# mLSTM scan of a two-block mixer: gate rows loaded from memory, the minimum on ScalarE, the next step's mask first, numerators in two pairs of banks in turn

## The chip, the cores and the metric

The kernel is one program on one core of a Trainium2 chip. The metric is the time of the whole program on the device in microseconds, as the median of several executions. Its engines are TensorE (PE in the profile, with PEld for its weight loads), VectorE (DVE), ScalarE (ACT), GpSimd (POOL) and SyncE (SP, which here only issues transfers). Each has a program of its own and they meet by semaphores. Every matmul writes to PSUM, eight banks of 2 KB a partition, called `ps` here.

## The reference

Two transformer blocks over 512 latent and 256 context tokens, in fp32. The change lies in the first mixer of the second block, in its mLSTM half: four heads of 128, in chunks of 128 tokens, once forward and once backward, the two results added. With the gates' logarithms given, a step of one direction is:

```
bcum = jnp.cumsum(fc, axis=-1)
d_log = jnp.where(lower, bcum[..., :, None] - bcum[..., None, :] + ic[..., None, :], -jnp.inf)
inter_log = bcum + m[..., None]
m_t = jnp.maximum(inter_log, jnp.max(d_log, axis=-1))
inter_w = jnp.exp(inter_log - m_t)
s = jnp.einsum('bhtd,bhsd->bhts', qc, kc) * jnp.exp(d_log - m_t[..., None])
num = inter_w[..., None] * jnp.einsum('bhtd,bhde->bhte', qc, c_mat) + jnp.einsum('bhts,bhse->bhte', s, vc)
den = inter_w * jnp.einsum('bhtd,bhd->bht', qc, n_vec) + jnp.sum(s, axis=-1)
h = num / jnp.maximum(jnp.abs(den), jnp.exp(-m_t))[..., None]
...
c_new = carry_w[..., None, None] * c_mat + jnp.einsum('bhs,bhsd,bhse->bhde', w, kc, vc)
n_new = carry_w[..., None] * n_vec + jnp.einsum('bhs,bhsd->bhd', w, kc)
```

## The kernel before, in words

The program is a series of blocks. Inside a block the engines run side by side; between two blocks all of them wait for one another. The second block's first projection (L1292) makes queries, keys, values and gates, unit by unit. While it runs, `Gates` turns the 16 gate columns into rows of 4 heads by 2 directions by 768 tokens and computes on them the running sums and maxima: `row_i` (for each token what stands for `inter_log - m_t`), `row_m` and `row_b`. TensorE then transposes them back to columns, per chunk (L3612), and after that goes on with the projection. The columns are `rp` (for each key token what is added to a query's row), `em`, `i_cols` and `w_all`.

The scan is a block of its own (L3799 and on), in twelve steps. `order_m` names direction `d` and chunk `c` of each; the directions alternate. In steps 0, 1 and 4 to 7 the chunk is met for the first time (`seen[s]` is false), in 2, 3 and 8 to 11 the other direction has been there. A step s goes so:

- TensorE (`front`): `bc`, the row of `row_i` of each head broadcast to all 128 partitions by a matmul of a broadcast column with the identity (L3804), and `cols`, the scores of keys and queries (L3811), into banks 0 and 1 or 2 and 3 by the parity of s.
- ScalarE: `iw`, the exponential of the broadcast rows (L3921). GpSimd multiplies the queries by it (`qs`, L3943) and the keys by `w_all` (`kw`, L3946).
- VectorE (`seg`): minimum of row plus `rp` column and zero (L3854, one for each head); ScalarE: exponential in place (`p_exp`, L3923); VectorE (`masked`): times the triangular mask (L3862), times the scores (L3865), `m`.
- TensorE (`p`): numerators and denominators, from the masked scores with the values (L3830) and from `qs` with the state (L3831), always into banks 4 and 5; then products for the state (`masked`, L3841) into banks 6 and 7.
- VectorE: the denominators, two operations and a reciprocal (L3878 to L3881, signalled as `rd`). If the chunk is new, ScalarE copies the numerators out with the reciprocal as scale (`give`, L3913); if not, VectorE adds them to what is there (L3886) and ScalarE squares the sum (L3790). Then VectorE brings the state forward (`mem`, L3898).

Each engine's instructions run in the order in which they are written. VectorE's order in iteration s is: minimum of s+1, denominators of s, addition of s, mask of s+1, state of s. ScalarE's is: `iw` of s, `p_exp` of s, `give` of s-1. TensorE's is: `front` of s+1, numerators of s, state products of s. Behind the last step ScalarE applies a sigmoid to the output gate (L3932) and loads the table of the square root (L3933). The next block is the band attention.

## Time and profile before

| | |
|---|---|
| median of 3 runs | 2406.1 us (2403.95 to 2406.68) |
| profiled execution, its own time | 2406.52 us |
| its span in the trace | 2404.7 us |
| TensorE busy | 2295.4 us (95%) |
| VectorE busy | 1256.0 us (52%) |
| ScalarE busy | 802.0 us (33%) |
| GpSimd busy | 971.5 us (40%) |
| mean granted TensorE clock | 0.98 |

The span is that of the trace, and the execution's own time has the start and end around it. Busy times count an engine's instructions without its waits; the busy share says little of a block whose engines wait for each other, so the block of the scan is read by itself, in the timeline and in windows. In a timeline row the first number is the start, the second the time from the start of the group's first instruction to the end of its last, and the bracket holds the idle time before it and the instruction that ended it. TensorE's fp32 matmuls show as two records each.

### The profile page before, as it was taken

The numbers are of one execution on the slowest core, as the hardware profiler recorded it, in microseconds if no ns is written. First come the engines' busy times: TensorE is split into PE (matmuls) and PEld (weight loads), VectorE is DVE, ScalarE is ACT, GpSimd is POOL, SyncE is SP. The second block draws the span as 40 slices with busy tenths as digits, with TensorE's granted clock in tenths as the row PEclk, the third lists the DMA queues.
The fourth block names the chain that finished last, engine by engine and source line by source line (L and its number), as shares of the span: only waits on it lengthen the run. The fifth ranks groups of instructions, "written<-read, shape, count | busy, mean of one in ns | idle before, by whom it ended". The sixth has DMA issues, their size and how long they took to land. (4 is left out here: it accounts for less than half of the span.)

```text
span 2404.7 us, 34304 instructions
## 1 busy us (share of the span) xinstructions
PE 2295.4 (95%) x14079; PEld 1901.3 (79%) x14079; DVE 1256.0 (52%) x2102; ACT 802.0 (33%) x1406; POOL 971.5 (40%) x639
## 2 busy tenths in 40 slices
PE   6999889999998999978999999999999998999999
PEld 5877757788776789855888888888877787888887
DVE  3647468756646660579165695755239651411111
ACT  4444353333325312356231121211143462322222
POOL 1236325555552222326234352534422133645653
PEclk8999989999999999989999999999999999999999
DMA  8325235535543111100112334343212002323321
GB/s 272 107 93 189 88 106 179 170 119 162 171 145 116 36 53 53 37 1 8 47 53 66 127 106 140 106 139 105 71 45 70 19 3 69 104 89 105 103 77 47
DMA packets 227577, 228.31 MB, mean 95 GB/s; under 512 B 7439, under 2 KB 225507, under 8 KB 227427
## 3 DMA queue, kind: packets, MB, share of 16 engines
q1 hardware_dynamic: 227091, 226.09, 29.4%
q8 instruction: 109, 1.79, 0.3%
q14 instruction: 41, 0.34, 0.0%
q10 hardware_dynamic: 336, 0.11, 0.0%
HBM read 224.08 MB, written 2.10 MB: 94 GB/s over the span
## 5 line engine op out<-in xcount | busy, mean ns | idle before, releaser
L1661 POOL TENSOR_TENSOR w_lo<-ring,w_hi 128x1024 fp32r<-128x1024 f32 x124 | 303.8, 2453 | 353.7 <-ACT w_hi L1655 353.7
L2633 DVE SCALAR_TENSOR_TENSOR xT<-ps,mods,xT 128x512 f32<-128x512 f32 (+1 forms) x160 | 107.6, 682 | 460.7 <-PE ps L1738 411.2
L1655 ACT ACTIVATE w_hi<-ring 128x1024 fp32r<-128x1024 f32 x124 | 130.7, 1058 | 490.9 <-PE ps L1738 490.9
L1736 PE MATMUL ps<-hidden_hi,w_hi 128*128 128x512 f32 (+1 forms) x768 | 272.6, 355 | 0.6 <-POOL hidden_lo L3023 0.6
L1737 PE MATMUL ps<-hidden_lo,w_hi 128*128 128x512 f32 (+1 forms) x768 | 272.0, 354 | 0.0
L2926 DVE SCALAR_TENSOR_TENSOR ffn_sums<-ps,cols,ffn_sums 128x441 f32<-128x441 f32 (+2 forms) x352 | 215.0, 687 | 108.9 <-ACT ffn_sums L2845 108.9
L1738 PE MATMUL ps<-hidden_hi,w_lo 128*128 128x512 f32 (+1 forms) x768 | 271.7, 354 | 0.0
L1736 PE MATMUL ps<-h_hi,w_hi 128*128 128x512 f32 (+1 forms) x720 | 255.5, 355 | 0.0
L1737 PE MATMUL ps<-h_lo,w_hi 128*128 128x512 f32 (+1 forms) x720 | 255.0, 354 | 0.0
L1738 PE MATMUL ps<-h_hi,w_lo 128*128 128x512 f32 (+1 forms) x720 | 254.7, 354 | 0.0
L2868 POOL TENSOR_TENSOR ffn_w_lo<-ring,ffn_w_hi 128x1024 fp32r<-128x1024 f32 (+2 forms) x76 | 161.7, 2130 | 215.8 <-ACT ffn_w_hi L2818 215.8
L1292 PE MATMUL ps<-h_hi,w_halves 128*128 128x512 f32 (+1 forms) x560 | 203.6, 364 | 7.6 <-DVE ab_lo L676 2.9
L3013 DVE TENSOR_TENSOR squares<-squares 128x512 f32<-128x512 f32 (+1 forms) x72 | 87.8, 1219 | 162.0 <-ACT squares L2999 162.0
L1271 POOL TENSOR_TENSOR ring_low<-ring,w_halves 128x1024 fp32r<-128x1024 f32 x31 | 74.7, 2417 | 228.4 <-ACT w_halves L1265 228.4
L1736 PEld LDWEIGHTS ps<-hidden_hi,w_hi 128*128 128x128 f32 x768 | 145.2, 189 | 22.3 <-POOL hidden_lo L3023 1.1
L1738 PEld LDWEIGHTS ps<-hidden_hi,w_lo 128*128 128x128 f32 x768 | 145.2, 189 | 20.2
L1737 PEld LDWEIGHTS ps<-hidden_lo,w_hi 128*128 128x128 f32 x768 | 145.2, 189 | 20.0
L2818 ACT ACTIVATE ffn_w_hi<-ring 128x1024 fp32r<-128x1024 f32 (+2 forms) x76 | 71.9, 947 | 250.5 <-PE ps L2807 234.3
L1736 PEld LDWEIGHTS ps<-h_hi,w_hi 128*128 128x128 f32 x720 | 136.1, 189 | 20.7 <-issue 1.2
L1737 PEld LDWEIGHTS ps<-h_lo,w_hi 128*128 128x128 f32 x720 | 136.2, 189 | 18.8
L1738 PEld LDWEIGHTS ps<-h_hi,w_lo 128*128 128x128 f32 x720 | 136.1, 189 | 18.9
L1068 DVE SCALAR_TENSOR_TENSOR h<-ring,sil,h 128x256 f32<-128x256 f32 x196 | 131.6, 695 | 5.0
(489 smaller groups left out, 5194.7 us busy)
## 6 DMA issues: line engine op xcount, KB each, us to landing
ring<-in_mlp_w SPq DMA_DIRECT2D x64, 1024.0 KB, 5.4
ring<-in_ada_w SPq DMA_DIRECT2D x48, 1024.0 KB, 5.4
ring<-in_w_ada SPq DMA_DIRECT2D x24, 1024.0 KB, 5.4
ring<-in_ffn_w_up SPq DMA_DIRECT2D x22, 1024.0 KB, 5.3
ring<-in_ab_w_in SPq DMA_DIRECT2D x11, 1024.0 KB, 5.3
ring<-in_ffn_w_down SPq DMA_DIRECT2D x12, 768.0 KB, 4.8
ring<-in_w_in SPq DMA_DIRECT2D x8, 1024.0 KB, 8.6
ring<-in_c_w_in SPq DMA_DIRECT2D x6, 1024.0 KB, 5.0
```

The source lines that it names most:

```text
L1068: ins = dve.scalar_tensor_tensor(acc, slab, s, acc, ALU.mult, ALU.add)
L1271: pool.tensor_tensor(low_half(h), ring_half(h), w_halves[:, h % 3, :, :].bitcast(F32), ALU.subtract)\
L1292: ins = pe.matmul(o, stationary, moving, start=(k == 0 and i == 0), stop=(k == KT - 1 and i == 2))
L1655: act.activation(w_hi[m][:, 0:x["kt"], :], ring[:, x["n"] % NS, 0:x["kt"], m * P:(m + 1) * P], ACT.Copy).then_inc(SW["w_hi"].sem, 1)
L1661: pool.tensor_tensor(w_lo[m][:, 0:x["kt"], :], ring[:, x["n"] % NS, 0:x["kt"], m * P:(m + 1) * P], w_hi[m][:, 0:x["kt"], :].bitcast(F32), ...
L1736: pe.matmul(o, w_hi[m][:, k, :], h, start=(k == 0), stop=False)
L1737: pe.matmul(o, w_hi[m][:, k, :], l, start=False, stop=False)
L1738: ins = pe.matmul(o, w_lo[m][:, k, :], h, start=False, stop=(k == x["kt"] - 1))
L2633: return nc.vector.scalar_tensor_tensor(x, bank, column_of(gates, t * 2 + 2 * gate + r), x, ALU.mult, ALU.add)
L2868: pool.tensor_tensor(w_lo[i % NW][:, 0:kt, :], ring[:, n % NS, 0:kt, m * P:(m + 1) * P], w_hi[i % NW][:, 0:kt, :].bitcast(F32), ALU.subtract)\
L2926: ins = dve.scalar_tensor_tensor(o, on_grid(ps[:, (first + m) % 4, :])[:, y0 + dy:y1 + dy, x0 + dx:x1 + dx], cols[:, CW + tap * 2 * FT + t ...
L3013: dve.tensor_tensor(sq, sq, sq, ALU.mult).then_inc(v_order.sem, 1)
```

## The change

The rows no longer come from TensorE. ScalarE's queue stores `row_i` to memory once, when the rows are complete; SP loads for each step the four heads' rows of the step's chunk into all 128 partitions, 256 KB a step, into six buffers in turn (`row_in`): two steps ahead of the last slab of the projection's stage, four at the block's start, and the rest as buffers come free. `iw` reads that buffer. The transposes of `row_i` and the column `i_cols` go; `rp_neg`, the negative of `rp`, takes its place. The minimum is made on ScalarE as Relu of (-row - rp), and the exponential takes its negative. VectorE's order becomes: mask of s+1, denominators of s, addition of s, state of s. Numerators of even steps go to banks 4 and 5, those of odd steps to 0 and 2, which the broadcasts have left. The squares are written into the row buffer as scratch. VectorE waits for the store before it sets the ones column of the values, which share memory with `row_i`.

```diff
@@ Gates
+        row_in = [big[:, rows_at + b * 512:rows_at + (b + 1) * 512].rearrange("p (h n) -> p h n", h=4)
+                  for b in (NR - 2, NR - 1, *range(NR - 2))]
+        def load_rows(sp, s):
+            d, c, _ = order_m[s]
+            sp.dma_start(row_in[s % NR], gate_rows[:, d, c * CH:(c + 1) * CH].partition_broadcast(P))\
+              .then_inc(row_loaded[s // 2 % (NR // 2)].sem, 16)
...
-                            for i, row in enumerate((row_m, row_b, row_i)):
+                            for i, row in enumerate((row_m, row_b)):
                                 pe.transpose(ps[:, 4, i * N4 + o:i * N4 + o + 4], row[:, d, cut], ident[0:4, 0:4])
...
                 elif (n, m) == (6, 0):
+                    self.wait(act, "gate_rows", 1)
+                    act.dma_start(gate_rows, row_i).then_inc(G["row_stored"].sem, 16)
                     self.wait(act, "gate_plain", 3)
...
                 self.wait(dve, "gate_cols", 1)
+                self.wait(dve, "row_stored", 16)
                 self.sig(dve.memset(va[:, :, :, P:P + 1], 1.0), "gate_plain")
                 self.sig(dve.tensor_copy(rp, ps[:, 4, 0:N4]), "gate_rp")
-                dve.tensor_copy(i_cols, ps[:, 4, 2 * N4:3 * N4])
+                dve.tensor_scalar(rp_neg, ps[:, 4, 0:N4], -1.0, None, ALU.mult)
@@ the scan, SP
+                for s in range(2, NR):
+                    load_rows(sp, s)
+                for s in range(NR, n_m):
+                    wait(sp, "p_exp", s // 2 * 2 - NR + 4)
+                    load_rows(sp, s)
@@ the scan, TensorE
-                    if s >= 2:
-                        wait(pe, "seg", s - 1)
-                        wait(pe, "iw", s - 1)
-                    for h in range(4):
-                        ins = pe.matmul(ps[:, 2 * (s % 2), h * P:(h + 1) * P],
-                                        heads_of(i_cols, d, c)[:, h:h + 1].to_broadcast([P, P]), ident,
-                                        start=True, stop=True)
-                    sig(ins, "bc")
...
-                    if s >= 1:
-                        wait(pe, "h", s)
                     if s >= 2:
+                        wait(pe, "h", s - 1)
                         wait(pe, "mem", s - 1)
                     for h in range(4):
-                        o = ps[:, 4 + h // 2, (h % 2) * 129:(h % 2) * 129 + 129]
+                        o = num_of(s)[:, h // 2, h % 2, :]
@@ the scan, VectorE
-                seg(0)
                 masked(0)
                 for s, (d, c, k) in enumerate(order_m):
                     if s + 1 < n_m:
-                        seg(s + 1)
-                    num = ps[:, 4:6, 0:258].rearrange("p b (h e) -> p b h e", h=2)
+                        masked(s + 1)
+                    num = num_of(s)
...
-                    if s + 1 < n_m:
-                        masked(s + 1)
@@ the scan, ScalarE
-                    wait(act, "bc", s + 1)
+                    d, c, _ = order_m[s]
+                    pair = row_loaded[s // 2 % (NR // 2)]
+                    act.wait_ge(pair.sem, pair.at(32 * (s // NR + 1)))
                     if s >= 2:
                         wait(act, "qs", s - 1)
-                    sig(act.activation(iws[s % 2], by_head(ps[:, 2 * (s % 2), :]), ACT.Exp), "iw")
-                    wait(act, "seg", s + 1)
-                    sig(act.activation(wide(pmats[s % 2]), wide(pmats[s % 2]), ACT.Exp), "p_exp")
+                    sig(act.activation(iws[s % 2], row_in[s % NR], ACT.Exp), "iw")
+                    if s >= 2:
+                        wait(act, "p", s - 1)
+                    for h in range(4):
+                        ins = act.activation(pmats[s % 2][:, h, :], row_in[s % NR][:, h, :], ACT.Relu,
+                                             bias=heads_of(rp_neg, d, c)[:, h:h + 1], scale=-1.0)
+                    a_order.step(act, ins)
+                    sig(act.activation(wide(pmats[s % 2]), wide(pmats[s % 2]), ACT.Exp, scale=-1.0), "p_exp")
```

Where the instructions stand. VectorE, iteration 5 of the scan, before: minimum of step 6 (L3854), denominators of step 5 (L3878 to L3881), mask of step 6 (L3862, L3865), state of step 5 (L3898).

```order
L3854 TENSOR_SCALAR hT<-ps,small 128x128 [waits p,iw,bc]
L3854 TENSOR_SCALAR hT<-ps,small 128x128 x3
L3878 TENSOR_TENSOR small<-ps,small 128x4 [waits h,p]
L3880 SCALAR_TENSOR_TENSOR small<-ps,small 128x4 [waits v_order]
L3881 RECIPROCAL small<-small 128x4 [waits v_order]
L3862 TENSOR_TENSOR hT<-hT,mats 128x512 [waits p_exp]
L3865 TENSOR_TENSOR hT<-hT,ps 128x512 [waits cols,v_order]
L3898 SCALAR_TENSOR_TENSOR rstd<-rstd,small,ps 128x129 [waits mem,masked]
L3898 SCALAR_TENSOR_TENSOR rstd<-rstd,small,ps 128x129 x3
```

The same iteration in the changed kernel: the mask of step 6 is L3875 and L3878, the denominators of step 5 are L3890 to L3893, the state is L3908.

```order
L3875 TENSOR_TENSOR hT<-hT,mats 128x512 [waits p_exp]
L3878 TENSOR_TENSOR hT<-hT,ps 128x512 [waits cols,v_order]
L3890 TENSOR_TENSOR small<-ps,small 128x4 [waits h,p]
L3892 SCALAR_TENSOR_TENSOR small<-ps,small 128x4 [waits v_order]
L3893 RECIPROCAL small<-small 128x4 [waits v_order]
L3908 SCALAR_TENSOR_TENSOR rstd<-rstd,small,ps 128x129 [waits mem,masked]
L3908 SCALAR_TENSOR_TENSOR rstd<-rstd,small,ps 128x129 x3
```

The minimum is gone, and the two operations of the mask, which wait for ScalarE's second exponential (`p_exp`), stand ahead of the denominators instead of behind them.

ScalarE, before, from the copies of step 5 (L3913) over the two exponentials of step 7 (L3921, L3923) to the copies of step 6.

```order
L3913 ACTIVATE hT<-ps,small 128x128 [waits rd]
L3913 ACTIVATE hT<-ps,small 128x128 x3
L3921 ACTIVATE hT<-ps 128x512 [waits qs,bc]
L3923 ACTIVATE hT<-hT 128x512 [waits seg]
L3913 ACTIVATE hT<-ps,small 128x128 [waits rd]
L3913 ACTIVATE hT<-ps,small 128x128 x3
```

The same place in the changed kernel: the copies are L3923, the exponential of the loaded row L3933, the four minimums L3937, the second exponential L3940.

```order
L3923 ACTIVATE hT<-ps,small 128x128 [waits rd]
L3923 ACTIVATE hT<-ps,small 128x128 x3
L3933 ACTIVATE hT<-big 128x512 [waits qs,rows_loaded0]
L3937 ACTIVATE hT<-big,small 128x128 [waits p]
L3937 ACTIVATE hT<-big,small 128x128 x3
L3940 ACTIVATE hT<-hT 128x512 [waits a_order]
L3923 ACTIVATE hT<-ps,small 128x128 [waits rd]
L3923 ACTIVATE hT<-ps,small 128x128 x3
```

The wait for VectorE's minimum (`seg`) has become four operations of ScalarE's own and a wait for their end (`a_order`), and the wait for the broadcast (`bc`) one for a transfer.

SP's queue in the changed kernel, from the projection's last slabs to the end of the scan. Before, it held here the slab loads alone, eleven of `in_ab_w_in` and four of `in_ab_w_out`.

```order
L326 DMA ring<-in_ab_w_in 128x8x256 [waits mm_done,mats_in]
L326 DMA ring<-in_ab_w_in 128x8x256 [waits mm_done] x10
L326 DMA ring<-in_ab_w_out 128x8x256 [waits mm_done] x3
L3589 DMA big<-gate_rows 128x4x128 [waits row_stored]
L3589 DMA big<-gate_rows 128x4x128
L326 DMA ring<-in_ab_w_out 128x8x256 [waits mm_done]
L1298 UNCONDITIONAL_BRANCH
L3820 UNCONDITIONAL_BRANCH [waits barrier_Pool_Activation_PE_DVE_SP_release]
L3589 DMA big<-gate_rows 128x4x128 x4
L3589 DMA big<-gate_rows 128x4x128 [waits p_exp] x6
```

Two row loads stand ahead of the last slab load, four at the block's start, and six wait for ScalarE.

## Rows read from the trace of the kernel before

**Rows 1.** Timeline, ScalarE and VectorE, first and last steps: start, us, engine, line.
```profile
984.11 0.60 ACT L3921 ACTIVATE hT<-ps 128x512 f32<-128x512 f32 x1 [1.59 <-PE ps L3804]
...
986.51 0.85 ACT L3927 ACTIVATE big<-ps 128x512 f32<-128x512 f32 x2
...
990.86 0.18 DVE L3881 RECIPROCAL small<-small 128x4 f32<-128x4 f32 x1
...
1038.46 0.18 DVE L3881 RECIPROCAL small<-small 128x4 f32<-128x4 f32 x1
...
1046.75 0.20 ACT L3933 ACTIVATE warm<-mats 128x1 f32<-128x1 f32 x1
```

**Rows 2.** Windows: us, busy PE, PEld, DVE, ACT, POOL (x), clock, DMA, GB/s.
```profile
1010.40:1028.30 17.90, 17.90 (x163) 17.90 (x162) 15.49 (x53) 9.47 (x24) 9.15 (x9) 1.00 0.01 1
1028.30:1038.70 10.40, 8.80 (x75) 8.22 (x73) 9.98 (x35) 4.78 (x20) 2.54 (x2) 1.00 0.01 2
```

**Rows 3.** Timeline, TensorE, from the broadcast of step 7 to that of step 8.
```profile
1014.96 1.06 PE L3804 MATMUL ps<-mats,small 128*128 128x128 f32 x8
1015.86 1.06 PE L3811 MATMUL ps<-big 128*128 128x128 f32 x8
1016.75 0.39 PE L3830 MATMUL ps<-big,hT 128*128 128x129 f32 x2
...
1019.43 0.83 PE L3804 MATMUL ps<-mats,small 128*128 128x128 f32 x6
```

**Rows 4.** Timeline, VectorE, from the denominators of step 5.
```profile
1014.27 0.16 DVE L3878 TENSOR_TENSOR small<-ps,small 128x4 f32<-128x4 f32 x1 [0.36 <-PE ps L3831]
...
1014.66 0.18 DVE L3881 RECIPROCAL small<-small 128x4 f32<-128x4 f32 x1
1014.76 0.66 DVE L3862 TENSOR_TENSOR hT<-hT,mats 128x512 f32<-128x512 f32 x1
1015.45 0.69 DVE L3865 TENSOR_TENSOR hT<-hT,ps 128x512 f32<-128x512 f32 x1
1016.06 1.12 DVE L3898 SCALAR_TENSOR_TENSOR rstd<-rstd,small,ps 128x129 f32<-128x129 f32 x4
1017.09 1.12 DVE L3854 TENSOR_SCALAR hT<-ps,small 128x128 f32<-128x128 f32 x4
```

**Rows 5.** Timeline, ScalarE, from the copies of step 5.
```profile
1014.88 1.14 ACT L3913 ACTIVATE hT<-ps,small 128x128 f32<-128x128 f32 x4 [0.30 <-DVE small L3881]
1016.05 0.60 ACT L3921 ACTIVATE hT<-ps 128x512 f32<-128x512 f32 x1
1018.25 0.63 ACT L3923 ACTIVATE hT<-hT 128x512 f32<-128x512 f32 x1 [1.60 <-DVE hT L3854]
```

**Rows 6.** Groups by line in 980 to 1045: count, busy us, mean ns, idle before.
```profile
L3913 ACT ACTIVATE hT<-ps,small 128x128 f32<-128x128 f32 x24 | 6.8, 367 | 2.8 <-DVE small L3881 2.8
...
L3790 ACT ACTIVATE squares<-hT 128x128 f32<-128x128 f32 x20 | 5.9, 297 | 6.8 <-DVE hT L3886 6.8
```

**Rows 7.** Timeline, ScalarE, in the attention behind the block.
```profile
1050.22 0.72 ACT L3486 ACTIVATE big<-big,small 128x513 f32<-128x513 f32 x1
```

**Rows 8.** Timeline, VectorE and ScalarE, step 8 (adding).
```profile
1028.28 1.13 DVE L3886 SCALAR_TENSOR_TENSOR hT<-ps,small,hT 128x128 f32<-128x128 f32 x4
...
1029.43 0.31 ACT L3790 ACTIVATE squares<-hT 128x128 f32<-128x128 f32 x1 [1.62 <-DVE hT L3886]
...
1030.62 0.57 ACT L3921 ACTIVATE hT<-ps 128x512 f32<-128x512 f32 x1
```

**Rows 9.** Gate preparation: TensorE's timeline and one window (columns as rows 2).
```profile
889.26 3.86 PE L3612 MATMUL ps<-mats,big 4*128 4x4 f32 x36 [2.94 <-DVE small L3718]
...
892.00:896.00 4.00, 4.00 (x24) 3.91 (x24) 0.42 (x4) 0.39 (x1) 0.00 (x0) 0.50 0.00 0
```

**Rows 10.** DMA issues: KB each, median us to landing.
```profile
out<-y_out SPq DMA_DIRECT2D x8, 256.0 KB, 2.8
```

**Rows 11.** Timeline, TensorE, ahead of the last step's numerators.
```profile
1041.18 0.49 PE L3830 MATMUL ps<-big,hT 128*128 128x129 f32 x2 [3.15 <-DVE hT L3865]
```

More of the change, by code:

```diff
@@ L207, in program @@
         v_order, a_order, g_order = order("v_order"), order("a_order"), order("g_order")
-        N = {n: tally("norm_" + n) for n in ("sum", "mean", "centered", "sq", "sq_used", "std", "scaled", "out", "hi", "lo", "lo_v", "recip", "spread", "spread_m")}
+        N = {n: tally("norm_" + n) for n in ("sum", "mean", "centered", "sq", "sq_used", "std", "scaled", "out", "hi", "lo", "recip", "spread", "spread_m")}
         FIRST_NORM = {n: tally("first_norm_" + n) for n in N}
@@ L1311, in _ @@
                         load_slabs(sp, slab_of(2) + 1)
+                        gates.sync(sp)
+                    load_slabs(sp, done[0] + NS - 1)
+                    if gates is not None and lead is None:
                         gates.sync(sp)
@@ L3572, in program @@
         dens = [small[:, 264 + 4 * i:268 + 4 * i] for i in range(2)]
-        i_cols = small[:, 272:272 + N4]
-        G = named("gate_logs", "gate_turned", "gate_kinds", "gate_plain", "gate_rows", "gate_cols", "gate_rp", "gate_sum")
+        rp_neg = small[:, 272:272 + N4]
+        gate_rows = nc.dram_tensor("gate_rows", (4, 2, TOK), F32, kind="Internal").ap()
+        NR = 6
+        row_loaded = [tally(f"rows_loaded{b}") for b in range(NR // 2)]
+        rows_at = free0 + 512
+        assert rows_at + NR * 512 <= 24576 and at_vb + KT * TOK <= rows_at + (NR - 2) * 512
+        row_in = [big[:, rows_at + b * 512:rows_at + (b + 1) * 512].rearrange("p (h n) -> p h n", h=4)
+                  for b in (NR - 2, NR - 1, *range(NR - 2))]
+        order_of = [[4, 5, 0, 1, 2, 3], [5, 4, 3, 2, 1, 0]]
+        order_m = [(d, order_of[d][k], k) for k in range(NCH) for d in range(2)]
+        def load_rows(sp, s):
+            d, c, _ = order_m[s]
+            sp.dma_start(row_in[s % NR], gate_rows[:, d, c * CH:(c + 1) * CH].partition_broadcast(P))\
+              .then_inc(row_loaded[s // 2 % (NR // 2)].sem, 16)
+        G = named("row_stored", "gate_logs", "gate_turned", "gate_kinds", "gate_plain", "gate_rows", "gate_cols", "gate_rp", "gate_sum")
         class Gates:
@@ L3614, in pe, with sync @@
                                        start=True, stop=True), "gate_cols")
+            def sync(self, sp):
+                self.wait(sp, "row_stored", 16)
+                for s in range(2):
+                    load_rows(sp, s)
             def pool(self, pool):
@@ L3772, in program @@
         used[0] = free0
-        part(4 * TOK, "p (k n) -> p k n", k=4)
         wide = lambda b: b.rearrange("p h n -> p (h n)")
@@ L3781, in program @@
         h_tok = hT[:, 0:4, :].rearrange("p t n -> p (t n)").rearrange("p (c h e) -> p c h e", c=NCH, h=4)
-        order_m = [(d, order_of[d][k], k) for k in range(NCH) for d in range(2)]
         seen = [any(x[1] == c for x in order_m[:s]) for s, (_, c, _) in enumerate(order_m)]
@@ L3786, in program, with chunk_squares, _ @@
         n_mem = n_m - 2
-        def chunk_squares(act, c):
+        num_of = lambda s: (ps[:, 4:6, :] if s % 2 == 0 else ps[:, 0:3:2, :])[:, :, 0:258].rearrange("p b (h e) -> p b h e", h=2)
+        def chunk_squares(act, c, junk=None):
             for h in range(4):
-                ins = act.activation(sq_junk[:, h * P:(h + 1) * P], h_tok[:, c, h, :], ACT.Square, accum_out=ssq[:, c, h:h + 1])
+                ins = act.activation(sq_junk[:, h * P:(h + 1) * P] if junk is None else junk[:, h, :], h_tok[:, c, h, :], ACT.Square, accum_out=ssq[:, c, h:h + 1])
             return ins
-        R = named("bc", "cols", "seg", "p_exp", "p", "m", "qs", "kw", "mem", "h", "iw", "rd", "masked", "swapped", "out_v")
+        R = named("cols", "p_exp", "p", "m", "qs", "kw", "mem", "h", "iw", "rd", "masked", "swapped", "out_v")
         with nc.Block() as block:
+            @block.sync
+            def _(sp):
+                for s in range(2, NR):
+                    load_rows(sp, s)
+                for s in range(NR, n_m):
+                    wait(sp, "p_exp", s // 2 * 2 - NR + 4)
+                    load_rows(sp, s)
             @block.tensor
@@ L3846, in _ @@
             def _(dve):
-                def seg(s):
-                    d, c, k = order_m[s]
-                    wait(dve, "bc", s + 1)
-                    wait(dve, "iw", s + 1)
-                    if s >= 2:
-                        wait(dve, "p", s - 1)
-                    for h in range(4):
-                        ins = dve.tensor_scalar(pmats[s % 2][:, h, :], ps[:, 2 * (s % 2), h * P:(h + 1) * P],
-                                                heads_of(rp, d, c)[:, h:h + 1], 0.0, ALU.add, ALU.min)
-                    sig(ins, "seg")
                 def masked(s):
@@ L3912, in give @@
                     for h in range(4):
-                        ins = act.activation(h_tok[:, c, h, :], ps[:, 4 + h // 2, (h % 2) * 129:(h % 2) * 129 + P],
+                        ins = act.activation(h_tok[:, c, h, :], num_of(s)[:, h // 2, h % 2, 0:P],
                                              ACT.Copy, scale=dens[s % 2][:, h:h + 1])
```

4 lines of the change are left out of this document (2 added, 2 removed).

## The prediction

> **What bounds the kernel now.** I read the page first, for what each engine does over the whole span. The change touches one block, the mLSTM scan, and the preparation of its gate rows some 95 us earlier, so I looked for the block by the lines of its instructions and read it engine by engine in the timeline. It runs from 983.0 to 1046.95 us: no engine works across its borders, so what it gains or loses moves everything behind it by as much. It has twelve steps. Write D(s) for the end of the reciprocal at L3881 in step s: D(0) = 991.04 and D(10) = 1038.64, 47.60 us apart [rows 1]. In the windows by stage TensorE is busy for all of 1010.40 to 1028.30 us, four steps of the first kind: a chunk that no direction has done yet, whose result ScalarE copies out ("first" steps: 0, 1 and 4 to 7). In the next window, two steps in which VectorE adds to a result that is there ("adding" steps: 2, 3, 8 to 11), VectorE is busy 9.98 of 10.40 us and TensorE 8.80 [rows 2]. So a first step is bound by TensorE: broadcast L3804 0.90, scores L3811 0.89, and numerators and state products together 2.68 (1016.75 to 1019.43), 4.47 in all [rows 3]. An adding step is bound by VectorE, two in those 10.40 us, 5.20 each [rows 2].
>
> **The change, part by part.** It takes the broadcast (0.90) off TensorE, and the minimum (L3854, four in 1.12 [rows 4]) off VectorE, which leaves TensorE 3.57 a step. Both bounds fall. But the minimum now stands on ScalarE between its two exponentials, and the masking of the next step stands on VectorE ahead of the denominators of this one. The order rows above show both, and together they close a loop that goes round once a step:
>
> D(s), then ScalarE's copy (or squares) of step s, then its exponential, minimum and second exponential of step s+2, then VectorE's two masking operations of step s+2, and only behind those the denominators of step s+1, which end in D(s+1).
>
> Each neighbour in this list is either behind the other in program order on one engine or waits for its semaphore, so nothing of it can overlap. In the kernel before, the masking stood behind the denominators, so the copy and the second exponential had the rest of the step to finish in, and ScalarE was idle for 1.6 us before L3923 [rows 5].
>
> The sizes of the loop in a first step:
> - wait of ScalarE for the reciprocal 0.04 (1014.84 to 1014.88), four copies 1.14 [rows 4, 5]
> - exponential of the loaded row: as L3923, 128x512 from SBUF, 0.63, less 0.10 of overlap [rows 5, 6]. The overlap: four copies of mean 367 ns take 1.14, so each starts some 0.1 before the last one ends.
> - minimum: four 128x128 operations from SBUF with a bias column. A square of this shape with fixed scale takes 0.297 [rows 6]; a column as bias costs 0.09 (0.72 for L3486 of 513 elements against 0.63 for L3923 of 512 [rows 5, 7]). So 0.38 each, 1.22 for four with three overlaps, less 0.10 behind the exponential. The trace has no such operation; bounds are 0.90 (as squares: the column free) and 1.52 (no overlap). I take 1.22, since both parts of it have a row.
> - 0.03 to wait for its own last operation, second exponential 0.63, 0.03 to VectorE
> - masking 1.38 (1014.76 to 1016.14), less 0.08 of overlap, and denominators 0.57 (1014.27 to 1014.84) [rows 4]
>
> That is 0.04 + 1.14 + 0.53 + 1.12 + 0.03 + 0.63 + 0.03 + 1.38 - 0.08 + 0.57 = 5.39 against 4.47. In an adding step the copies give way to VectorE's additions and ScalarE's squares: 0.04 + 1.13 + 0.02 + 1.19 (L3790 at 1029.43 to L3921 at 1030.62, overlap included) [rows 8], then 0.63 + 1.12 + 0.03 + 0.63 + 0.03 + 1.38 - 0.08 + 0.57: 6.69 against 5.20. TensorE's 3.57 and VectorE's longest load, 1.30 + 0.57 + 1.17 + 1.04 = 4.1, fit inside with room, and so does GpSimd, idle most of the time.
>
> Ten rounds lie between D(0) and D(10): six of first steps (0, 1, 4 to 7) and four of adding steps (2, 3, 8, 9). 6 x 5.39 + 4 x 6.69 = 59.1, against 47.6: **+11.5 us**.
>
> A rule speaks against the move by itself. The trace prices four minimums at 1.12 on VectorE and at 1.22 by my working on ScalarE, a loss of 0.10 x 10 = 1 us if nothing else happened. The Trainium skill (ScalarE: Activation LUTs, Rules for kernel authors) says to use VectorE, not ScalarE, for relu, max and min. By that rule alone the step would lose about this 1 us; by the rows the engine hardly matters, and it is the place in the loop that costs. The same page (What ACT_TABLE_LOAD costs) gives an activation with a column as bias 280 ns + 0.833 ns an element and an overlap of 93 ns, an estimate of 1.27 for the four, which would make the sum 0.6 us larger; no run here has shown it yet.
>
> **The two pairs of banks.** They let step s+1's numerators start before the result of step s is taken. In the loop above the numerators of step s+1 are ready 1.9 after its masking, and wait for nothing; they are not in the loop. I cost the banks at nothing, gain or loss. Only the last two steps profit, and ScalarE's tail hides that: D(10) to the end of its last activation is 8.3 us (1038.64 to 1046.95), of additions, squares, two table loads and sigmoids [rows 1]. The change leaves all of it, so the tail stays 8.3.
>
> **The start.** ScalarE no longer waits for TensorE's first broadcast: its first exponential began at 984.11 after an eightfold L3804 of 1.06 [rows 1, 3], so it may now begin at 983.0. Then 0.63 + 1.12 + 0.03 + 0.63, the two copies of step 0 (0.85 - 0.10 [rows 1]), 0.53 + 1.12 + 0.03 + 0.63 for step 1, then 0.03 + 1.38 - 0.08 + 0.57: D(0) at 990.4 against 991.04, **-0.7**.
>
> **The gate rows.** TensorE's transposes at L3612, 36 in 3.86 us, stand behind a wait of 2.94 for VectorE and in front of the next projection [rows 9]. Twelve of them go: **-1.3**, at most; as little as 0 if the clock, which has fallen to 0.50 there [rows 9], comes back at the same moment anyway. The new store of 24 KB leaves ScalarE's queue at 889.2. VectorE now waits for it with its memset, rp and w_all behind it, and ScalarE's copies of the projection behind the memset. The nearest store lands in 2.8 [rows 10], so at 892.0, before the shortened transposes end (892.3). If it came later, TensorE has four banks in turn to work into, so I cost it at nothing.
>
> **SP's queue.** Two row loads of 256 KB stand behind the wait for that store and ahead of the last projection slab's refill, which is not due before the last unit ends, over 80 us later: nothing. The other four loads of the first round start with the block. At 2.8 each, one after another, the second pair lands at 988.6, and ScalarE reaches it at D(0) + 1.2 = 991.6. Later pairs have two steps, 11 us. Nothing.
>
> Sum: 11.5 - 0.7 - 1.3 = +9.5. The profiled execution took 2406.5, 0.4 above the median of 2406.1 of the three shown; with the sum 2416.0, and against the median **2415.6**.
>
> **Rivals.**
> - The engines overlap, and the step follows the busiest: TensorE 3.57 in first steps, VectorE 4.1 in adding ones, 6 x 3.57 + 4 x 4.1 = 37.8, so -9.8 - 0.7 - 1.3: 2394.3. For it: TensorE is full in first steps [rows 2]. Against it: it needs D(s+1) not to wait for ScalarE's work of step s+2, which the order forbids. It decides only from a loop under 4.47 and 5.20, and that would need the masking out of it. 0.05.
> - The loop is there but shorter: minimums at 0.90 and the full 1.3 at the gates give 2411.8 (twelve groups in the path, 3.8 less), and a little more overlap brings it within 0.2%. 0.08.
> - The clock. It stayed at 1.00 over TensorE's idle 3.15 us before 1041.18 [rows 11], and was at half after 2.94 us of idle that only four-column transposes followed [rows 9]. In the new loop TensorE idles 1.8 us in a first step and 3.1 in an adding one, between 3.57 of full work. If it fell for the whole block, TensorE's 7.14 a step would be the bound: 71.4 - 47.6 - 2.0 = +21.8, 2427.9. In adding steps alone it would cost only 4 x 0.45. 0.05.
> - The forecast: 0.82.
>
> **Range.** The minimum's bounds move the sum by 3.8 down and 3.6 up, the transposes by 1.3 up. That is 2411.8 to 2420.5; a part of the case within 0.2% comes in below: 2410.0 to 2420.5. A measurement of this kernel can't tell less than about 0.2% (4.8 us) from no change. Slower means over 2410.9: the forecast and the clock, 0.86; same 0.08; faster 0.06.
>
> **What the profile after would show.** The reciprocals 5.4 apart in first steps and 6.7 in adding ones; VectorE idle for 2.4 to 2.6 before the first masking operation and released by ScalarE's second exponential; no idle of ScalarE before that exponential; TensorE idle before each group of numerators, released by the masking; four minimums in 1.2; 24 transposes in 2.6. Reciprocals 3.6 to 4.5 apart would prove the loop wrong; idle of ScalarE before the first exponential, released by a DMA, would mean late rows; a granted clock near half between 985 and 1045 would be the third rival.

## The result and the profile after

The change makes the kernel slower. Its median is 2422.97 us (5 runs, 2419.6 to 2426.19) against 2406.1 for the kernel before, 5 runs of it beside them; the ratio is 1.0071, 95% interval 1.0061 to 1.0082. The forecast was 2415.6, and its range ended at 2420.5: the sign and the loop were right, the size was too small by 7.4 us.

The scan's block decides it. The reciprocal is at L3893 now, and the rows that answer to [rows 1] are these: ScalarE's first exponential, the reciprocals of step 0 and of step 10, and ScalarE's last activation.

```profile
979.83 0.63 ACT L3933 ACTIVATE hT<-big 128x512 f32<-128x512 f32 x1 [0.40 <-PEq L3768]
...
987.62 0.18 DVE L3893 RECIPROCAL small<-small 128x4 f32<-128x4 f32 x1
...
1050.06 0.18 DVE L3893 RECIPROCAL small<-small 128x4 f32<-128x4 f32 x1
...
1058.35 0.20 ACT L3950 ACTIVATE warm<-mats 128x1 f32<-128x1 f32 x1
```

D(0) is 987.80 and D(10) 1050.24: 62.44 us apart, against 47.60 before and 59.1 forecast. The tail from D(10) to the end of the last activation is 8.31, as before. The reciprocals stand 5.80 apart in first steps; in adding steps they stand 7.09 apart from D(2) to D(4), and 6.75 from D(8) to D(10).

One round trip of the kernel after, in a first step (timeline, all engines, TensorE's shown only where it starts):

```profile
1016.57 1.04 POOL L3963 TENSOR_TENSOR big<-big,small 128x512 f32<-128x512 f32 x1
1017.12 1.04 DVE L3875 TENSOR_TENSOR hT<-hT,mats 128x512 f32<-128x512 f32 x1 [2.50 <-ACT hT L3940]
1018.19 0.69 DVE L3878 TENSOR_TENSOR hT<-hT,ps 128x512 f32<-128x512 f32 x1
1018.80 0.15 DVE L3890 TENSOR_TENSOR small<-ps,small 128x4 f32<-128x4 f32 x1
1018.93 0.49 PE L3854 MATMUL ps<-big,hT 128*128 128x129 f32 x2 [1.95 <-DVE hT L3878]
...
1019.18 0.18 DVE L3893 RECIPROCAL small<-small 128x4 f32<-128x4 f32 x1
...
1019.39 1.14 ACT L3923 ACTIVATE hT<-ps,small 128x128 f32<-128x128 f32 x4 [2.31 <-DVE small L3893]
...
1020.41 0.65 ACT L3933 ACTIVATE hT<-big 128x512 f32<-128x512 f32 x1
...
1020.93 1.28 ACT L3937 ACTIVATE hT<-big,small 128x128 f32<-128x128 f32 x4
...
1022.24 0.63 ACT L3940 ACTIVATE hT<-hT 128x512 f32<-128x512 f32 x1
1022.36 1.04 POOL L3963 TENSOR_TENSOR ada_rows<-big,small 128x512 f32<-128x512 f32 x1
...
1022.90 1.04 DVE L3875 TENSOR_TENSOR hT<-hT,mats 128x512 f32<-128x512 f32 x1 [2.50 <-ACT hT L3940]
```

Read it from the reciprocal (ends 1019.36) downwards: copies, exponential of the loaded row, minimum, second exponential, masking, each starting where the one above it ends, until VectorE comes back to the denominators. That is the round trip of the prediction, link by link. VectorE waits 2.50 ahead of the masking for ScalarE (2.4 to 2.6 was forecast), ScalarE waits 2.31 for VectorE, and TensorE waits 1.95 for the masking. No engine is full: in the window over four first steps, D(4) to D(8), and in that over two adding steps, D(8) to D(10) (columns as in [rows 2]), none reaches 75% of the stretch.

```profile
1013.57:1036.74 23.17, 17.00 (x130) 16.24 (x129) 12.74 (x37) 13.78 (x40) 9.07 (x8) 0.93 0.12 37
1036.74:1050.24 13.50, 6.12 (x49) 5.58 (x48) 7.90 (x26) 7.19 (x28) 2.55 (x2) 0.97 0.01 2
```

One thing in the round trip is not as forecast: the first masking operation takes 1.04 where [rows 4] has 0.66. It lies beside GpSimd's product of keys and weights, L3963. In step 10, where GpSimd has no such product to make, the same line reads:

```profile
1041.59 0.69 DVE L3875 TENSOR_TENSOR hT<-hT,mats 128x512 f32<-128x512 f32 x1 [2.66 <-ACT hT L3940]
```

At the gates, TensorE's transposes (L3630, 24 of them) and VectorE's wait for the new store, which answer to [rows 9]:

```profile
888.40 2.23 PE L3630 MATMUL ps<-mats,big 4*128 4x4 f32 x24 [1.43 <-DVE small L3744]
...
891.19 0.18 DVE L3685 COPY small<-ps 128x48 f32<-128x48 f32 x1 [2.85 <-DMA gate_rows<-big]
...
979.85 1.13 PE L3836 MATMUL ps<-big 128*128 128x128 f32 x8 [0.83 <-PEq L3768]
```

The last row is TensorE's first of the block, 3.1 us earlier than before (982.94, where the prediction had 983.0 rounded).

### The profile page after: what moved, and what is told of

It is laid out like the page before. It is cut to its first block and busy times, and to the rows that moved or that the text cites. A ratio compares the mean times of both kernels' runs of the same rounds, so it can differ in the third digit from the quotient of the medians.

```text
span 2421.1 us, 34080 instructions
## 1 busy us (share of the span) xinstructions
PE 2293.6 (95%) x13971; PEld 1897.0 (78%) x13971; DVE 1248.1 (52%) x2054; ACT 816.4 (34%) x1454; POOL 974.6 (40%) x639
## 5 line engine op out<-in xcount | busy, mean ns | idle before, releaser
L1292 PE MATMUL ps<-h_hi,ring_low 128*128 128x512 f32 (+1 forms) x384 | 135.3, 352 | 0.0
```

The costliest lines, as they stand in the source:

```text
L1292: ins = pe.matmul(o, stationary, moving, start=(k == 0 and i == 0), stop=(k == KT - 1 and i == 2))
```

## The experiments

Ten variants, and both kernels once more, in three batches, each batch beside runs of the kernel before (medians 2404.55, 2403.56 and 2404.67). Diffs are against the changed kernel. D(0) to D(10) is read from the profiled execution of each.

| kernel | D(0) to D(10) | median us | ratio to before, 95% interval |
|---|---|---|---|
| e4_give_late | 37.46 | 2395.8 | 0.9964 [0.9951, 0.9978] |
| e1_mask_last | 45.01 | 2400.43 | 0.9985 [0.9976, 0.9994] |
| e10_mask_last_one | 45.18 | 2402.99 | 0.9995 [0.9986, 1.0005] |
| e12_give_one | 47.52 | 2405.16 | 1.0004 [0.9995, 1.0013] |
| r2_before_again | 47.60 | 2403.52 | 0.9994 [0.9985, 1.0004] |
| e13_give_min_dve | 52.50 | 2410.52 | 1.0027 [1.0017, 1.0037] |
| e6_min_dve | 53.12 | 2411.05 | 1.0027 [1.0018, 1.0036] |
| e5_rows_only | 54.98 | 2412.3 | 1.003 [1.0019, 1.0042] |
| e2_kw_late | 59.69 | 2420.35 | 1.0067 [1.0053, 1.0081] |
| r1_after_again | 62.45 | 2420.93 | 1.007 [1.0054, 1.0085] |
| e3_one_pair | 62.47 | 2425.51 | 1.0087 [1.0073, 1.0101] |
| e11_rows_port | 63.08 | 2421.86 | 1.0065 [1.0051, 1.008] |

The time follows the block, though loosely: from the first row to r1_after_again the block grows by 25.0 us and the median by 25.1, but the median less the block's ten rounds runs from 2355.4 (e1) to 2363.0 (e3), so that a difference of a few us in the time says little of the block.

### e1_mask_last: the mask of the next step behind the denominators

> The changed kernel with one thing moved back: VectorE makes the mask of step s+1 behind the denominators and additions of step s. Theory of the loop (copy or squares of s, exponential, minimum, exponential of s+2, mask of s+2, denominators of s+1, all in a row): the mask and the second exponential leave the loop; D(0) to D(10), 62.4 us in the changed kernel, comes to 43 to 45, and the time to 2403 (2400 to 2407). Rival, the load of ScalarE: the minimum on ScalarE is what costs, and it stays, so D(0) to D(10) stays over 58 and the time over 2418.

```diff
-                    if s + 1 < n_m:
-                        masked(s + 1)
                     num = num_of(s)
...
                         sig(ins, "h")
+                    if s + 1 < n_m:
+                        masked(s + 1)
```

Measured: 45.01, 17.4 less than the changed kernel, with first steps of about 4.02 and adding ones of 5.20. Timeline of a first step:

```profile
1013.76 0.63 ACT L3940 ACTIVATE hT<-hT 128x512 f32<-128x512 f32 x1
...
1014.72 0.18 DVE L3891 RECIPROCAL small<-small 128x4 f32<-128x4 f32 x1
1014.82 0.66 DVE L3875 TENSOR_TENSOR hT<-hT,mats 128x512 f32<-128x512 f32 x1
1014.93 1.14 ACT L3923 ACTIVATE hT<-ps,small 128x128 f32<-128x128 f32 x4 [0.54 <-DVE small L3891]
```

The second exponential ends at 1014.39, before the reciprocal does at 1014.90, so the mask behind it waits for nothing. The place of the mask is the cause: everything else of the change together is worth a small gain over the kernel before (45.01 against 47.60).

The adding steps still take 5.20, as in the kernel before, although the minimum has left VectorE. One adding step, and the window from D(8) to D(10):

```profile
1025.47 0.49 PE L3854 MATMUL ps<-big,hT 128*128 128x129 f32 x2 [1.36 <-DVE hT L3878]
...
1027.56 0.16 DVE L3888 TENSOR_TENSOR small<-ps,small 128x4 f32<-128x4 f32 x1 [1.11 <-PE ps L3855]
```

```profile
1022.93:1033.33 10.40, 7.07 (x59) 6.50 (x57) 7.90 (x27) 7.20 (x28) 2.56 (x3) 1.00 0.01 2
```

VectorE is busy for 7.90 of 10.40 us and waits for the numerators, and they wait for the mask. So what holds an adding step at 5.20 is a second round trip, of additions, mask, numerators and denominators, and not VectorE's load, as the prediction read it from [rows 2]. The minimum stood in a wait of that round trip. A mask ahead of the denominators opens this second round trip and closes the first.

### e2_kw_late: GpSimd's product of keys made to wait for the masking

> The changed kernel; only GpSimd's product of keys and weights of step s waits until VectorE has masked step s, so that GpSimd is still while VectorE makes the first masking operation. Theory that this operation took 1.04 instead of 0.66 us because GpSimd was at work beside it: it returns to 0.69, the ten rounds lose 0.36 each in eight of them, D(0) to D(10) 59.5, the time 2420 (3 less than the changed kernel). Rival: the operation is slower because of the row loads that write SBUF or because of the wait for the exponential; it stays at 1.04 and the time at 2423.

```diff
+                    wait(pool, "m", s + 1)
                     sig(pool.tensor_tensor(kws[s % 2], k_tok
```

Measured: 59.69, steps of 5.44 and 6.76 (5.39 and 6.69 were forecast for the changed kernel). VectorE and GpSimd in one step:

```profile
1012.10 0.69 DVE L3875 TENSOR_TENSOR hT<-hT,mats 128x512 f32<-128x512 f32 x1 [2.67 <-ACT hT L3940]
...
1013.59 1.04 POOL L3964 TENSOR_TENSOR ada_rows<-big,small 128x512 f32<-128x512 f32 x1 [2.02 <-DVE hT L3878]
```

The first masking operation is back at 0.69 and the block loses 2.75 us by a wait that was added. The medians of the whole program (2420.35 here, 2422.97 and 2420.93 for the changed kernel) can't separate so little; the block can. Of the 3.3 us by which the block was longer than forecast, all but 0.6 was GpSimd's product beside the masking.

### e3_one_pair and e10_mask_last_one: one pair of banks for all numerators

> The changed kernel with all numerators in banks 4 and 5 again, and TensorE waiting for the result of step s-1. Theory of the loop: the banks are not in it; D(0) to D(10) stays 62.4, only the last step is 1.6 us later and hidden by ScalarE's tail; the time stays 2423. Rival: the second pair of banks hides numerators and copies; without it each step is longer by 0.5 us or more, 2428 or over.

> The mask of the next step behind the denominators and the additions, as in the run with the mask last, and one pair of banks for all numerators: what are the two pairs worth once the round trip is open? Theory (banks nothing in this order): from one reciprocal the four copies (1.2), the numerators (1.8 to 1.9) and the denominators (0.57) make 3.6 to 3.7, less than the 4.02 that the first steps took with two pairs, and in adding steps VectorE is full either way. D(0) to D(10) 45.0, time within 0.1% of the 2400.4 of that run. Rival (the second pair is what opens the round trip): first steps back at 4.5 or more, 48 to 50 us between D(0) and D(10), 2404 to 2406. Beside the run of the rows only (2412.3) it prices the minimum alone, since the two differ in nothing else: the minimum on ScalarE is then worth some 12 us.

```diff
-        num_of = lambda s: (ps[:, 4:6, :] if s % 2 == 0 else ps[:, 0:3:2, :])[...
+        num_of = lambda s: ps[:, 4:6, :][...
...
+                    if s >= 1:
+                        wait(pe, "h", s)
```

e3 is the changed kernel with one pair; e10 has the mask last as well. Measured: 62.47 against 62.44, and 45.18 against 45.01. The second pair is worth nothing in the block in either order, as theory had it. The medians are some 2.5 us above those of their partners (2425.51 against 2422.97, 2402.99 against 2400.43); the intervals of the ratios overlap, and the 2.5 us are not in the ten rounds.

### e4_give_late: copies and squares of a step one iteration later on ScalarE

> The changed kernel, only that ScalarE takes the result of step s-2 instead of s-1 behind the second exponential of step s (the squares go to the scratch of the kernel before). The mask stays ahead of the denominators. Theory of the loop: the copy of step s no longer stands between D(s) and the exponentials of step s+2, the loop is open, and the next limits are TensorE 3.6 a step and VectorE 4.0 in adding steps: D(0) to D(10) 36 to 39 and the time 2398 (2394 to 2402). Rival, the load of ScalarE or of its minimum: no change, over 2418.

```diff
-                        chunk_squares(act, c, row_in[s % NR])
+                        chunk_squares(act, c, None if s != 10 else row_in[4])
...
-                    if s >= 1:
-                        give(s - 1)
+                    if s >= 2:
+                        give(s - 2)
+                give(n_m - 2)
```

ScalarE now does exponential, minimum and exponential of step s+2 before the copies of step s, so D(s) no longer stands ahead of them. (The squares' unused output goes to another place, since the row is read later now.) The mask is still first. Measured: 37.46, steps of 3.57 and 4.00, and 2395.8 us, faster than both kernels. These are the overlapped bounds of the first rival (3.57 and 4.1). Windows over four first steps, D(4) to D(8), and over two adding steps, D(8) to D(10):

```profile
1006.62:1021.02 14.40, 14.40 (x132) 14.40 (x131) 13.98 (x37) 14.07 (x42) 10.06 (x9) 1.00 0.15 43
1021.02:1029.02 8.00, 6.29 (x54) 5.94 (x53) 7.72 (x26) 5.33 (x23) 1.28 (x1) 1.00 0.01 3
```

TensorE is full in first steps, and VectorE is all but full in adding ones. So the mask ahead of the denominators is harmless as long as ScalarE has the second exponential ready; only together with ScalarE's own order did it close a loop. It is more than harmless: with both round trips open the ten rounds take 7.5 us less than with the mask last (e1). This kernel also shows how long a masking operation can take at no cost in a first step, where TensorE is the bound:

```profile
1007.50 1.04 POOL L3964 TENSOR_TENSOR big<-big,small 128x512 f32<-128x512 f32 x1
1007.58 1.51 DVE L3875 TENSOR_TENSOR hT<-hT,mats 128x512 f32<-128x512 f32 x1
...
1011.07 1.04 POOL L3964 TENSOR_TENSOR ada_rows<-big,small 128x512 f32<-128x512 f32 x1
1011.25 1.41 DVE L3875 TENSOR_TENSOR hT<-hT,mats 128x512 f32<-128x512 f32 x1
```

The product ends at 1008.54 and the mask at 1009.09; in the second pair 1012.11 and 1012.66; in the changed kernel 1017.61 and 1018.16. The mask ends 0.55 behind GpSimd's product whenever it starts beside it, whether it has then run for 1.04, 1.41 or 1.51. It is not slowed, it is held until the product is over.

### e12_give_one: the best order with one pair of banks

> The best order so far (copies and squares of a step one iteration later, mask still first) with one pair of banks for all numerators. Theory (in this order the second pair is what keeps TensorE going): the numerators of step s+1 then wait for the copies of step s, which stand behind exponential, minimum and exponential of step s+2 on ScalarE: numerators 1.8, the three 2.5, copies 1.15, 5.4 to 5.5 in a first step; adding steps, where VectorE gives the banks free, stay at 4.0 to 4.1. D(0) to D(10) about 49, 11 to 12 us more than with two pairs, 2407. Rival (banks are worth nothing in any order): 37.5 and 2396.

Measured: 47.52, 10.1 us more than e4, first steps 5.28 to 5.29 behind the first, adding ones 4.05 with one of 4.77; 2405.16, where 49 and 2407 were expected. TensorE's numerators wait for the copies:

```profile
1014.99 1.13 ACT L3924 ACTIVATE hT<-ps,small 128x128 f32<-128x128 f32 x4
...
1016.37 0.46 PE L3855 MATMUL ps<-big,hT 128*128 128x129 f32 x2 [1.48 <-ACT hT L3924]
```

The two pairs of banks, worth nothing in e3 and 0.2 us in e10, are worth 10 us here.

### e5_rows_only and e6_min_dve: the minimum back on VectorE, reading the loaded row

> Of the change only the loaded rows: the minimum is back on VectorE (reading the loaded row), VectorE's order is the old one, and all numerators are in banks 4 and 5. Theory: the broadcast leaves TensorE (3.6 a step), so the limit of a first step becomes VectorE's 4.1 to 4.2 and that of an adding step stays VectorE's 5.1 to 5.2: D(0) to D(10) 45 to 46 against 47.6 before, D(0) itself up to 1.5 earlier, and 1 to 3 at the gate transposes: 2400 (2397 to 2403). Rival: the loads or their waits cost something by themselves, and the time is 2405 or over.

> The changed kernel with the minimum back on VectorE, ahead of the next mask; the mask stays ahead of the denominators, rows loaded, two pairs of banks. Theory of the loop: the loop stays closed and is shorter by the minimum only (1.2 less on ScalarE in each round, while VectorE makes its 1.0 to 1.1 beside ScalarE's copies, partly in the loop): D(0) to D(10) 52 to 56, the time 2411 to 2416, still slower than before. Rival, the minimum on ScalarE is what costs: D(0) to D(10) under 48 and the time 2405 or less.

```diff
+                seg(0)
                 masked(0)
...
+                    if s + 1 < n_m:
+                        seg(s + 1)
...
-                    for h in range(4):
-                        ins = act.activation(pmats[s % 2][:, h, :], row_in[s % NR][:, h, :], ACT.Relu, ...
...
+                    wait(act, "seg", s + 1)
```

Here `seg` is four minimums on VectorE, from `row_in`. e6 has this edit alone; e5 also has the mask last and one pair of banks, so that only the loaded rows remain of the change. Measured: e6 53.12, 9.3 less than the changed kernel; e5 54.98, where a gain over the kernel before was expected, and 2412.3 us. The theory for e5 fell: fewer matmuls, and slower. VectorE's minimum is the reason. In e6 and in e5, with GpSimd's products:

```profile
1016.24 0.87 DVE L3878 TENSOR_SCALAR hT<-big,small 128x128 f32<-128x128 f32 x4
...
1017.05 1.28 POOL L3969 TENSOR_TENSOR hT<-big,hT 128x512 f32<-128x512 f32 x1 [2.08 <-ACT hT L3947]
...
1017.81 1.07 DVE L3886 TENSOR_TENSOR hT<-hT,mats 128x512 f32<-128x512 f32 x1 [0.70 <-ACT hT L3949]
1018.29 1.49 POOL L3972 TENSOR_TENSOR ada_rows<-big,small 128x512 f32<-128x512 f32 x1
```

```profile
1018.16 1.27 POOL L3970 TENSOR_TENSOR hT<-big,hT 128x512 f32<-128x512 f32 x1 [2.76 <-ACT hT L3948]
1018.93 1.97 DVE L3879 TENSOR_SCALAR hT<-big,small 128x128 f32<-128x128 f32 x4
1019.39 1.04 POOL L3973 TENSOR_TENSOR ada_rows<-big,small 128x512 f32<-128x512 f32 x1
...
1020.93 0.63 ACT L3950 ACTIVATE hT<-hT 128x512 f32<-128x512 f32 x1 [2.86 <-DVE hT L3879]
```

Four minimums take 0.87 in e6, where they are as good as over when GpSimd begins (less than the 1.12 from PSUM in [rows 4]), and 1.97 in e5, where they start inside one product and meet the next. Single ones take 0.27 to 1.08 in e5, with a median of 0.28: most are quick and a few are held. It goes both ways: in e6 the mask is held until 0.55 behind the first product, and the second product then takes 1.49 instead of 1.04.

### e11_rows_port: e5 with both products behind the masking

> The kernel of the rows-only run (minimum on VectorE from the loaded row, mask last, one pair), with both of GpSimd's products made to wait until the two masking operations of their step are done. Theory (VectorE's minimum reads SBUF and shuts out GpSimd, and is shut out by it): no GpSimd product lies beside the minimum, so four take 1.12 and not 1.97, and the longest single one is under 0.3 us instead of 1.08. The time hardly gains by it, since the numerators now wait 1.27 for the first product: steps of about 5.15 and 6.2, 55.7 between D(0) and D(10), 2411 to 2414. Rival (the minimum from SBUF with a column is slow by itself): single minimums stay over 0.4 us on the mean, four in 1.9, and the steps get longer than 6.

```diff
                     wait(pool, "iw", s + 1)
+                    wait(pool, "m", s + 1)
```

Measured: 63.08, four minimums still 1.92. The experiment missed its aim: the products moved, and the state updates kept VectorE from the minimum until they were running, so that it lay beside them again. Timeline:

```profile
1019.41 1.26 POOL L3971 TENSOR_TENSOR hT<-big,hT 128x512 f32<-128x512 f32 x1 [3.17 <-issue]
1020.23 1.92 DVE L3879 TENSOR_SCALAR hT<-big,small 128x128 f32<-128x128 f32 x4
1020.63 1.04 POOL L3974 TENSOR_TENSOR big<-big,small 128x512 f32<-128x512 f32 x1
```

The last four minimums, which no second product follows, take 1.12, and the first four, with GpSimd idle, 0.87. So the rival (slow by itself) falls all the same, on this and on e6. The block's time, over 7 us more than the 55.7 expected, says nothing on it.

### e13_give_min_dve: the best order with the minimum on VectorE

> The best order so far with the minimum of step s+2 on VectorE, right behind the denominators of step s, so that it stands in nobody's round trip. What is the minimum on ScalarE worth in the best order? Theory (VectorE becomes the bound): 1.38 + 0.57 + 1.04 + 1.12 = 4.1 in first steps, 5.15 in adding ones, 45 to 46 between D(0) and D(10), 8 us more than with ScalarE's, 2404. If the minimum or the mask waits for one of GpSimd's products in each step, up to 1 us a step more: 50 to 55, 2409 to 2413. Rival (the engine of the minimum does not matter when it is out of the round trip): 37.5, 2396.

Measured: 52.50, 15.0 us more than e4, and 2410.52: the second branch of what was expected, 50 to 55. Over three steps VectorE is busy for 15.43 of 15.70 us, and part of that is being held (2.46 for four minimums beside two products):

```profile
1012.40:1028.10 15.70, 11.61 (x100) 11.12 (x99) 15.43 (x39) 6.54 (x18) 6.90 (x7) 1.00 0.15 42
```

The minimum on ScalarE is worth 15 us in the best order, and 10 where the mask is last (e5 against e10, where 12 were expected). By the sum in the expectation 8 of the 15 are VectorE's load, which leaves 7, an estimate, for its being held beside GpSimd; no run separates the two. In the changed kernel, where ScalarE stands in the loop, the minimum there costs 9.3 (e6).

### r1_after_again and r2_before_again: both kernels once more

> The changed kernel itself, once more, for its TensorE clock outside the scan. If the 4.8 us that it lost behind the scan in its first trace (two stretches at half clock, around 1155 and 1790 us) come from where the clock happens to stand in this execution, other stretches show now; if they belong to the program, the same two show again.

> The kernel before, once more, for its TensorE clock outside the scan: as many stretches at half clock behind the scan as in its first trace (three from 1200 us on without the last, 17 us of half clock in all) if they belong to the program; others if they come from the execution. Its time 2404 to 2406.

Measured: 2420.93 (4 runs) and 2403.52 (10 runs), D(0) to D(10) 62.45 and 47.60. The block repeats to 0.01 us. What stands behind it does not: from the end of the block to the first store of y_out the changed kernel took 1333.56 in one profiled execution and 1329.19 in the other, the kernel before 1328.74 and 1330.89. Counted from the block's end, the same matmuls of the changed kernel come 1.5 us later than those of the kernel before at about 1780 us, and 4.8 later at about 1830. The windows over 1780 to 1800 us show the stretch between; first the changed kernel, then the same kernel again:

```profile
1780.00:1800.00 20.00, 16.96 (x159) 14.62 (x159) 15.23 (x34) 8.30 (x14) 0.00 (x0) 0.74 0.08 27
```

```profile
1780.00:1800.00 20.00, 16.20 (x176) 14.04 (x175) 14.27 (x32) 7.79 (x13) 0.00 (x0) 1.00 0.09 27
```

The granted clock is 0.74 there in one execution and 1.00 in the other. Neither expectation came out whole. The changed kernel shows its stretches near 1155 and 2020 again, without those near 1235, 1790 and 1820; the kernel before shows its stretches near 1220, 1800 and 2000 again, with one more near 1140. The places repeat, and which of them go to half clock differs from one execution to the next.

## Why the prediction was wrong

Against the profiled execution of before (2406.52) the changed one took 2422.97, +16.45, where +9.5 was forecast. The difference of 6.95, by the prediction's own terms:

| term | forecast | measured | miss |
|---|---|---|---|
| ten rounds, D(0) to D(10) | +11.5 | +14.84 | +3.3 |
| start of the block to D(0) | -0.7 | -0.15 | +0.55 |
| all ahead of the block, gate rows among it | -1.3 | -3.1 | -1.8 |
| tail | 0 | 0 | 0 |
| behind the block | 0 | +4.85 | +4.85 |

Two terms failed: the masking inside the loop, and the nothing behind the block. Without either miss the time would have been within the range (some 2420.2 or 2418.1 against 2420.5).

**The round trip** was right link by link: the order, the waits on three engines, its independence of the banks (e3) and its cause (e1 takes away 17.4 us, e4 25.0). **The term that failed in it is the masking**, put at 1.38 from a row of [rows 4] in which GpSimd was idle; it took 1.76 (1017.12 to 1018.88). Moving the mask put it 0.5 us behind the start of GpSimd's product in every step that has one: 8 x 0.35 = 2.8 of the 3.3, and e2 shows 2.75 of it. The rest is the minimum, 1.27 where 1.22 was taken: 10 x 0.05 = 0.5, and here the estimate from the Trainium skill (ScalarE: Activation LUTs, What ACT_TABLE_LOAD costs) was the better one (1.27; four took 1.26 to 1.28). The trace of before had one warning that I did not read, in the first step, from the timeline of VectorE and GpSimd:

```profile
986.01 1.04 POOL L3946 TENSOR_TENSOR big<-big,small 128x512 f32<-128x512 f32 x1
986.63 0.96 DVE L3862 TENSOR_TENSOR hT<-hT,mats 128x512 f32<-128x512 f32 x1 [0.69 <-ACT hT L3923]
```

The same line takes 0.96 here and ends at 987.59, 0.54 behind the product. The largest of a line's durations, and what GpSimd did beside it, would have given 1.04 for the moved mask and a loop of 5.8. The Trainium skill states it (SBUF — State Buffer, "SBUF: two separate sides"): VectorE and GpSimd share a pair of ports under an exclusive lock, also for a VectorE operation with two inputs in SBUF against a GpSimd operation that reads SBUF, and the loser is blocked fully. By that rule, the trace agrees, but for 0.1 us: the mask ends 0.55 behind the product in all ten such steps, where a mask that did nothing before the product's end would end 0.66 to 0.69 behind it.

**The start** fell short by the same two things (1.05 for the second mask, 1.27 twice for the minimums) and by copies of 0.87 for 0.75.

**The gates** are not contradicted. From the first transpose to the first matmul of the block the kernel before took 93.68 and 92.18 in its two profiled executions, and the twelve profiled executions with 24 transposes took 91.42 to 91.65: 0.5 to 2.3 us, forecast 1.3. In the pair compared it was 2.2. The store ended VectorE's wait at 891.19, and TensorE went on with its projection without a wait. The other 0.9 of the 3.1 is there when the transposes start (888.40 against 889.26); in the repeated runs they start at 890.16 and 888.55, and in the twelve anywhere from 888.36 to 892.45. This part is of the execution, and it was luck that it hid some of the other misses.

**Behind the block** nothing was forecast, on the ground that what the block gains or loses moves everything behind it by as much. In the profiled execution 4.85 us came, the largest single miss. The stretch around the half clock near 1790 us holds 3.3 of it, and the same kernel ran without it in r1. Still it is not a matter of one execution alone: the medians are 16.9 and 17.4 us apart in the two batches that have both kernels, and rounds, start and gates make only 12.4 to 14.2 of it. The medians of e4, e10 and e12 also lie 1 to 4 us above what these parts give for them. The changed kernel's executions range from 2419.6 to 2426.19, and the mean clock of each falls as the time rises (0.978 at 2419.6, 0.975 at 2426.19). The prediction's third rival asked for the clock inside the block only; one stretch of it there (the 0.93 in the window above) cost nothing, since the steps around it are 5.80 like the others. **Open** is why the slower kernels have such a stretch more often: of the profiled executions with over 52 us between D(0) and D(10), five of eight had one of 6.8 us or more near 1790, and of the four with less than the kernel before none; no run varied it by itself. So the cause of this miss stays open.

**The banks, the loads and the clock inside the block** cost nothing, as said. **The first rival** (2394.3) was not what this change does, but it named the bounds: e4 reaches 3.57 and 4.00 and 2395.8 us. The prediction's remark that the engine of the minimum hardly matters by the rows was wrong, since it is worth 9.3 to 15 us one way or the other. And an adding step of the kernel before was not bound by VectorE's load but by its own round trip (e1); no term of the sum rests on that. The chances as listed give 0.87 for slower and 0.05 for faster, where the range paragraph has 0.86 and 0.06.

## What to carry to other kernels

Before moving a step, write down the loop from an engine's result back to itself through all engines' program orders; a mask that is harmless in one order (e4) closes the loop in another. Two pairs of banks are worth nothing or 10 us depending on it, and the minimum on ScalarE costs 9 us or saves 10 to 15. An engine that is busy for nearly all of a step, as VectorE in [rows 2], may still only fill the waits of a round trip: take its work away and see whether the step gets shorter (e1). Take the duration of a moved VectorE operation from a row in which GpSimd is as busy beside it as it will be, and look at the longest of a line, not at a typical one. When a VectorE operation beside a GpSimd one is long, subtract the other's end: a constant remainder points to its being held, and moving GpSimd's operation (e2) gives the time back.

## What the runs showed of the hardware

- A 128x512 product of VectorE with both inputs in SBUF takes 0.66 to 0.69; started inside a GpSimd product of 1.04 that reads SBUF, it ends 0.55 behind it (1.04, 1.41 and 1.51 in all). The same holds beside the product of queries (0.88 in e12). The second masking operation, one input in PSUM, was 0.69 in every run, beside a GpSimd product too (e12).
- Four 128x128 subtract-and-minimum operations from SBUF take 0.87 on VectorE with GpSimd idle, 1.12 from PSUM [rows 4], 1.1 to 1.6 when they meet one GpSimd product (e5, e11, e13) and 1.9 to 2.8 when they meet two. On ScalarE, as relu with a column as bias, they took 1.26 to 1.28 in every run, beside a GpSimd product (the changed kernel) or mostly clear of one (e12).
- GpSimd is held as well: its product took 1.49 instead of 1.04 where VectorE's mask was waiting in front of it (e6, e12).
